# Four changes of order in a two-block layer stack on one Trainium2 core: MLA's keys, the first loads, a norm sum, GLA's outputs

## The chip, the core and the metric

The kernel runs on one core of one Trainium2 chip. The time is that of one execution on the device, in microseconds (us). Three runs of the kernel before took 3557.26, 3553.92 and 3555.59 us; the median is 3555.59.

TensorE multiplies, VectorE (DVE) and ScalarE (ACT) work elementwise, GpSimd (POOL) too, and SyncE (SP) asks for the transfers. Each engine works through its own list in order; between engines there are only semaphores.

## What is computed

One sequence of 256 positions, 2048 channels, float32. Two blocks of two layers each:

```python
for i in range(2):                                   # first block
    z = rmsnorm(x, g_mix[i]) @ w_in[i]               # 4928 columns, in 12 parts
    y_a = mla_group(zq, zkv, zkr, ...)               # 4 heads; q, k of 128 + 64 (rotated), both RMS-normed
    y_b = sc_b * causal_dwconv(sc_c * sc_h, w_sc[i])             # 3 taps
    y_c = silu(layernorm(causal_dwconv(cf_a * sigmoid(cf_g), w_cf[i])))  # 31 taps
    y_d = retention_group(rq, rk, rv, rg, ...)
    x = x + concatenate([y_a, y_b, y_c, y_d]) @ w_o[i]
    uf = causal_dwconv(rmsnorm(x, g_ffn[i]) @ w_up[i], w_ffn_conv[i])    # 2 x 5632 columns
    x = x + (silu(gate) * up) @ w_down[i]
    x = x + (p[i] @ w_pe[i]) * sigmoid(rmsnorm(x, g_pe[i]) @ w_pg[i])
for l in range(2):                                   # second block
    p = rms_norm(x, norm_g) @ w_in                   # forgetting, differential, block and gated linear attention
    x = x + concatenate([fox, diff, moba, gla]) @ w_out
return rms_norm(x, final_norm_g)
```

MLA's queries and keys come from low-rank parts: `c_q = rmsnorm(zq)`, `c_kv = rmsnorm(zkv)`, `q = c_q @ w_q_up`, `kv = c_kv @ w_kv_up`; a key is 128 channels of its head and 64 rotated ones that all heads share, normed together.

## The kernel before

**Slabs.** All lies with channels on the 128 partitions and positions along the row: x is 16 chunks of 128 x 256. A projection is cut into *slabs*: 128 output channels by all input channels, 128 x 2048 numbers, 1 MB. Each float32 operand is used as a rounded high half and a residue. ScalarE rounds a slab (`split_hi`, L1027, tile `whi`), VectorE subtracts (`split_lo`, L1394, tile `wlo`), and TensorE does 16 pairs of matmuls: the high weights by both halves of H (512 columns, L548) and the low weights by H's high half (256 columns, L552). Slabs whose source is not split this way use three matmuls of 256 columns (L550 to L552). H holds the normed input: ScalarE writes its high half (`x_hi`, L1060), VectorE its low half (`x_lo`, L1444). The norm's factor is not in H: the sum over channels is a matmul with ones (`norm_sum`, L586), ScalarE takes the root (`norm`, L1047), VectorE inverts it (`inverse`, L1433) and multiplies every output by it. The squares of x for this sum are made and added by GpSimd, chunk by chunk (`square_sum`, L438 and L443).

**Order.** There is no planner: the order is written out by hand. A slab's turn on each engine is one step of `run`. SyncE loads slab n into one of four places when slab n - 4 is done. In its turn of slab n VectorE first takes the output of slab n from its PSUM bank (L1411 adds the two halves of 512 columns, L1419 multiplies), then makes the residue of slab n + 3 (`AHEAD` is 3), and only then does what hangs on the step number. ScalarE rounds slab n + 3 first. Beside the slabs, the small work of attention hangs on the step s (the slab's number in the layer): on TensorE `behind_first(l, s)` behind slab s and `within_first` in its middle, on ScalarE `beside_first`, on VectorE `before_first` and `after_first` (before and behind the residue). The second block has the same four under the names `after_slab`, `within_slab`, `beside_slab`, `before_split` and `after_split`.

**Steps of the first block.** zq and zkv are s = 0 to 5, zkr 6, cfg 7 to 10, cfa 11 to 14, kv 15, qn 16, qr 17, ret 18 to 25, sc 26 to 37, rg 38 to 41. Behind slab 6 TensorE sums the squares for the low-rank norms (`lora_sums`, L627). Behind qn it sums the keys' squares, ScalarE takes a root, VectorE inverts (`invert(8)`, L1437), and behind qr TensorE spreads the inverse norms over partitions (`spread`, L635); VectorE then scales the keys (`keys_scaled`) and turns the queries (`query_turned`), and the scores of the four heads lie behind slabs 19 to 22. Between these VectorE does 62 steps of two of the four 31-tap convolutions (`cf_taps`, L1532), a few in each slab; GpSimd does the other two (L485, L488) from cfa's third slab on.

**The start.** SyncE asks for x's first quarter, slab 0, x's other three quarters and then slabs 1 to 3. ScalarE rounds slab 0, writes H, and rounds slabs 1 and 2; VectorE follows. `setup` (VectorE) works out the angles of the rotation and the sums for lambda in stages, `set_up` (ScalarE) takes sines and exponentials, `setup_end` finishes.

**pe and pg.** p @ w_pe fills eight banks (`both_units`); ScalarE copies six of them (L1346), VectorE two. Then comes the norm sum and the 16 slabs of pg, in a loop.

**gla.** Behind slabs 13 to 16 and 18 to 21 of the second block TensorE multiplies eight levels of decayed keys and queries (`gla_levels`, first instruction L764), for which VectorE makes differences (L1719), ScalarE two exponentials (`level_exps`, L1204 and L1205) and GpSimd four products (L504, L505). `gla_take` (ScalarE, L1221 and L1222) copies the outputs of the first pair out of four PSUM banks, which the second pair's levels use next.

## Time and profile before

| | |
|---|---|
| median of three runs | 3555.59 us (3553.92 to 3557.26) |
| profiled execution | 3560.03 us, span 3558.2 us |
| mean granted TensorE clock | 0.983 |
| TensorE busy | 97% of the span |
| VectorE, ScalarE, GpSimd busy | 75%, 41%, 28% |
| DMA | 605 MB, mean 170 GB/s |

The span runs from the first to the last instruction. Times of the rows below are us from the start of the span. A busy share is an average over stages with different limits; what counts is where TensorE, which is busy nearly all the time, waits.

### The profile page before, as it was taken

To read this page: it belongs to the slowest core of one execution; us is meant where nothing else is said; L and a number is where in the kernel's file an instruction comes from. 1 tells how busy PE (TensorE), PEld (TensorE's weight loads), DVE (VectorE), ACT (ScalarE), POOL (GpSimd) and SP (SyncE) were. 2 spreads that over 40 slices of the span, in tenths; PEclk is the share of its full clock that TensorE was granted. 3 is DMA by queue.
4 is the path that set the end of the run, shared out by engine and by line. 5 is a ranking of instruction groups with operands and counts; after the bars stand their busy time and mean duration, and the time that the engine had idled before them with its cause. 6 is when DMAs were issued, how large, how long until landed. Compare 5 with 4: busy or idle time off the path is not lost. (4 is left out here: it accounts for less than half of the span.)

```text
span 3558.2 us, 55706 instructions
## 1 busy us (share of the span) xinstructions
PE 3448.0 (97%) x21150; PEld 3027.4 (85%) x21150; DVE 2653.3 (75%) x3438; ACT 1476.1 (41%) x1494; POOL 1008.0 (28%) x794
## 2 busy tenths in 40 slices
PE   6999999999999999999999999999999999999998
PEld 5899888888888888998888888888878888878887
DVE  6876688777786778766887787867767776677775
ACT  3434444343333543344443434335444444444442
POOL 3470433212122434805232121214331004140004
PEclk8999999999999999999999999999999999999999
DMA  4334455555545544344555555555443445444453
GB/s 183 136 132 165 171 189 190 178 195 177 199 171 188 184 171 141 132 156 175 189 189 176 200 174 195 178 187 190 168 154 141 147 174 183 164 145 142 154 178 142
DMA packets 90062, 605.08 MB, mean 170 GB/s; under 512 B 10000, under 2 KB 10160, under 8 KB 28592
## 3 DMA queue, kind: packets, MB, share of 16 engines
q1 hardware_dynamic: 88992, 599.83, 47.9%
q10 hardware_dynamic: 912, 3.12, 0.2%
q8 instruction: 103, 1.69, 0.2%
q14 instruction: 55, 0.45, 0.0%
HBM read 600.81 MB, written 2.10 MB: 169 GB/s over the span
## 5 line engine op out<-in xcount | busy, mean ns | idle before, releaser
L548 PE MATMUL bank<-H,whi 128*128 128x512 f32 x6784 | 2425.6, 401 | 56.4 <-DVE H L1444 40.8
L552 PE MATMUL bank<-H,wlo 128*128 128x256 f32 x7552 | 2130.2, 282 | 0.0
L548 PEld LDWEIGHTS bank<-H,whi 128*128 128x128 f32 x6784 | 1285.3, 189 | 378.1 <-DVE wlo L1394 36.2
L1027 ACT ACTIVATE whi<-raw 128x2048 fp32r<-128x2048 f32 (+1 forms) x610 | 1095.3, 1796 | 1181.9 <-DMA raw<-in_slabs_down 267.3
L1394 DVE TENSOR_TENSOR wlo<-raw,whi 128x2048 fp32r<-128x2048 f32 (+1 forms) x610 | 1338.6, 2195 | 189.8 <-ACT whi L1027 185.8
L552 PEld LDWEIGHTS bank<-H,wlo 128*128 128x128 f32 x7552 | 1441.9, 191 | 0.4
L548 PE MATMUL bank<-G,whi 128*128 128x512 f32 x1408 | 494.6, 393 | 0.0
L465 POOL TENSOR_TENSOR sqtmp<-tmp 128x256 f32<-128x256 f32 x88 | 219.0, 2489 | 891.4 <-DVE tmp L1957 891.4
L552 PE MATMUL bank<-G,wlo 128*128 128x256 f32 x1408 | 398.2, 283 | 0.0
L548 PEld LDWEIGHTS bank<-G,whi 128*128 128x128 f32 x1408 | 264.4, 188 | 61.0
L552 PEld LDWEIGHTS bank<-G,wlo 128*128 128x128 f32 x1408 | 264.7, 188 | 0.0
L1411 DVE TENSOR_REDUCE z<-bank 128x256 f32<-128x512 f32 x148 | 102.1, 690 | 171.1 <-PE bank L552 169.8
L438 POOL TENSOR_TENSOR sqtmp<-x 128x256 f32<-128x256 f32 x135 | 150.0, 1111 | 272.8 <-DVE x L1463 203.8
L443 POOL TENSOR_TENSOR sqacc<-sqacc,sqtmp 128x256 f32<-128x256 f32 x135 | 222.8, 1650 | 10.6
L550 PE MATMUL bank<-H,whi 128*128 128x256 f32 x768 | 224.3, 292 | 0.0
L551 PE MATMUL bank<-H,whi 128*128 128x256 f32 x768 | 218.6, 285 | 0.0
L1411 DVE TENSOR_REDUCE tmp<-bank 128x256 f32<-128x512 f32 x208 | 143.6, 691 | 92.2 <-PE bank L552 90.0
L1462 DVE TENSOR_TENSOR x<-x,bank 128x256 f32 (+1 forms) x192 | 80.8, 421 | 163.6 <-PE bank L552 163.5
L1336 ACT ACTIVATE G<-sqtmp 128x256 f32 (+1 forms) x88 | 36.8, 418 | 400.1 <-POOL sqtmp L465 400.1
L438 POOL TENSOR_TENSOR sqacc<-x 128x256 f32<-128x256 f32 x9 | 17.1, 1895 | 604.1 <-DVE x L1463 558.8
L485 POOL TENSOR_TENSOR sqtmp<-z,cols 128x256 f32<-128x256 f32 (+30 forms) x124 | 120.0, 968 | 191.0 <-DVE z L1905 181.3
L550 PEld LDWEIGHTS bank<-H,whi 128*128 128x128 f32 x768 | 148.6, 193 | 3.8 <-issue 2.7
(314 smaller groups left out, 2503.7 us busy)
## 6 DMA issues: line engine op xcount, KB each, us to landing
raw<-in_slabs_up SPq DMA_DIRECT2D x176, 1024.0 KB, 4.8
raw<-in_slabs_down SPq DMA_DIRECT2D x128, 704.0 KB, 4.1
raw<-in_slabs_wo SPq DMA_DIRECT2D x32, 1024.0 KB, 4.8
raw<-in_slabs_pg SPq DMA_DIRECT2D x32, 1024.0 KB, 4.8
raw<-in_slabs_gates SPq DMA_DIRECT2D x32, 1024.0 KB, 4.8
raw<-in_slabs_wout SPq DMA_DIRECT2D x32, 1024.0 KB, 4.7
raw<-in_slabs_sc SPq DMA_DIRECT2D x24, 1024.0 KB, 4.8
raw<-in_slabs_fox SPq DMA_DIRECT2D x24, 1024.0 KB, 4.8
```

The lines of the kernel that those rows point to most:

```text
L438: pool.tensor_tensor((sqtmp if c else sqacc)[:], x[:, c, :], x[:, c, :], ALU.mult).then_inc(S("pool_sq"), 1)
L443: ins = pool.tensor_tensor(sqacc[:], sqacc[:], sqtmp[:], ALU.add)
L465: pool.tensor_tensor(act_f[:], tmp[:, 3, :], tmp[:, 2, :], ALU.mult).then_inc(S("act_f32"), 1)
L485: pool.tensor_tensor(sqtmp[:, s:T], u[:, 0:T - s], w, ALU.mult).then_inc(S("cf_product"), 1)
L548: pe.matmul(b[0:r.m, :], whi[:, n % RAW, w], r.src[:, k, :], start=at == 0, stop=False)
L550: pe.matmul(b[0:r.m, 0:T], whi[:, n % RAW, w], r.src[:, k, 0:T], start=at == 0, stop=False)
L551: pe.matmul(b[0:r.m, 0:T], whi[:, n % RAW, w], r.src[:, k, T:2 * T], start=False, stop=False)
L552: last = pe.matmul(b[0:r.m, 0:T], wlo[:, n % RAW, w], r.src[:, k, 0:T], start=False, stop=at == r.kt - 1)
L1027: act.activation(whi[:, n % RAW, 0:w], raw[:, n % RAW, 0:w], ACT.Copy).then_inc(S("hi_ready"), 1)
L1394: dve.tensor_tensor(wlo[:, n % RAW, 0:w], raw[:, n % RAW, 0:w], whi[:, n % RAW, 0:w].bitcast(F32), ALU.subtract).then_inc(S("lo_ready"), 1)
L1411: return dve.tensor_reduce(dst, b[0:m, :].rearrange("p (h t) -> p t h", h=2), AX, ALU.add)
L1462: link_in_loop(dve.tensor_tensor(xc, xc, b[:, 0:T], ALU.add), i, j)
```

## The change

1. **MLA.** `spread` and `keys_scaled` move from s = 17 to 18, `query_turned` from 18 to 19, and scores, masks, exponentials, probabilities and outputs of the four heads by one slab. `key_rope`, with its matmul, moves from s = 9 to 13. Four of VectorE's taps leave slab 18.
2. **Start.** Slab 0 is asked for ahead of x. ScalarE squares x in four instructions, VectorE adds them in three, and the norm sum takes four matmuls over y; GpSimd has no part in this first sum. Slab 3 is rounded and split before the first step. p, lambda and positions are loaded into z instead of y. The stages of `setup` hang on s = 2 to 11, one each; ScalarE's `set_up` moves from s = 6 to 12 and `setup_end` from 7 to 13.
3. **pg.** The norm sum, the root and the reciprocal come behind pg's first slab; pg's first four slabs are written out instead of being the loop's first turn.
4. **gla.** ScalarE's `gla_take` comes ahead of `level_exps` in the same step.
5. The packed vectors have 1006 columns instead of 1024.

```diff
@@ SyncE
+        sp.dma_start(raw[:, 0, :], runs[0].slabs[0]).then_inc(S("raw0"), 16)
         for k in range(4):
             sp.dma_start(x[:, 4 * k:4 * k + 4, :].rearrange("p c t -> p (c t)"),
                          d["x"][:, 4 * k * T:(4 * k + 4) * T]).then_inc(S(f"x_in{k}"), 16)
-            if k == 0:
-                sp.dma_start(raw[:, 0, :], runs[0].slabs[0]).then_inc(S("raw0"), 16)
@@ GpSimd
-        square_sum(lambda c: (S(f"x_in{c // 4}"), 16))
@@ TensorE
         def norm_sum():
             k = nth("norm")
-            pe.wait_ge(S("square_sum"), k)
+            if k == 1:
+                pe.wait_ge(S("x_squares"), 3)
+                for c in range(4):
+                    last = pe.matmul(pX[:, 0:T], ones[:], y[:, c, :], start=c == 0, stop=c == 3)
+                last.then_inc(S("norm_sum"), 1)
+                return
+            pe.wait_ge(S("square_sum"), k - 1)
...
+        def gate_norm(l):
+
+            yield
+            pe.wait_ge(S("pe_taken"), 6 * l + 3)
+            pe.wait_ge(S("evac"), by["pe", l].first + 1)
+            norm_sum()
+            yield
...
-            if 21 <= s < 25:
-                weighted(12 + s - 21, 4 * l + 1 + (s - 21) // 2)
+            if 22 <= s < 26:
+                weighted(12 + s - 22, 4 * l + 1 + (s - 22) // 2)
...
-            if s == 9:
+            if s == 13:
                 pe.wait_ge(S("turn_gains"), l + 1)
                 pe.wait_ge(S("evac"), by["zkr", l].first + 1)
                 turn_halves(vtok[:, 0:P], [small[:]], pO)
...
-            if s == 17:
+            if s == 18:
                 spread([((pX, pX, pO, pO)[h][:, (h % 2) * T + t * P:(h % 2) * T + (t + 1) * P], 4 * t + h)
...
-            if 19 <= s < 23:
-                h = s - 19
+                h = s - 20
...
-            pe.wait_ge(S("pe_taken"), 6 * l + 3)
-            pe.wait_ge(S("evac"), by["pe", l].first + 1)
-            norm_sum()
-            run(("pg", l), h_ready(hbase), free=lambda j, l=l: pe.wait_ge(S("pe_taken"), 6 * l + 4 + min(j, 2)))
+            run(("pg", l), h_ready(hbase), gate_norm(l), free=lambda j, l=l: pe.wait_ge(S("pe_taken"), 6 * l + 4 + min(j, 2)))
@@ ScalarE
+            if ahead and isinstance(i, int) and n + 4 * i == AHEAD:
+                return
...
+            if s in (17, 22):
+                gla_take(l, (s - 17) // 5)
             if 16 <= s < 20:
                 level_exps(8 * l + 4 + s - 16)
-            if s in (17, 22):
-                gla_take(l, (s - 17) // 5)
...
         split_hi(r0, 0, 2, 0)
+        for k in range(4):
+            act.activation(y[:, 4 * k:4 * k + 4, :], x[:, 4 * k:4 * k + 4, :], ACT.Square).then_inc(S("x_square"), 1)
+        split_hi(r0, 0, 3, 0)
         norm()
...
-            norm()
             for i, j in run(("pg", l)):
+                if isinstance(i, int) and i == 0 and j == 0:
+                    norm()
@@ VectorE
-                advance(taps, 4 if 4 * i + j in (0, 6, 7) else 0)
+                advance(taps, 4 if 4 * i + j in (6, 7) else 0)
...
-            if l == 0 and s < 6:
-                advance(setting, 2)
-            if l == 0 and s == 5:
+            if l == 0 and 2 <= s < 12:
+                advance(setting, 1)
+            if l == 0 and s == 11:
                 finish(setting)
-            if l == 0 and s == 7:
+            if l == 0 and s == 13:
                 setup_end()
+            if s == 13:
+                key_rope(l)
...
             if s == 9:
-                key_rope(l)
                 lora_low(l)
...
-            if s == 17:
+            if s == 18:
                 keys_scaled(l)
-            if s == 18:
+            if s == 19:
                 query_turned(l)
...
         split_lo(r0, 0, 2, 0)
+        for a, b, n in ((0, 4, 2), (8, 12, 4), (0, 8, 0)):
+            dve.wait_ge(*((S("x_square"), n) if n else (S("x_squares"), 2)))
+            dve.tensor_tensor(y[:, a:a + 4, :], y[:, a:a + 4, :], y[:, b:b + 4, :], ALU.add).then_inc(S("x_squares"), 1)
+        split_lo(r0, 0, 3, 0)
         inverse()
...
-            inverse()
             for i, j, b in run(("pg", l)):
                 k = 4 * i + j
+                if isinstance(i, int) and i == 0 and j == 0:
+                    inverse()
```

## Rows read from the trace of the kernel before

**Rows 1.** The page, busy time, share of the span and instructions of each engine.

```profile
PE 3448.0 (97%) x21150; PEld 3027.4 (85%) x21150; DVE 2653.3 (75%) x3438; ACT 1476.1 (41%) x1494; POOL 1008.0 (28%) x794
```

**Rows 2.** Busy time of each engine from 440 to 1170 us, TensorE's clock, DMA.

```profile
440.00:1170.00 730.00, 730.00 (x4168) 637.06 (x4167) 573.21 (x716) 284.99 (x239) 171.99 (x114) 1.00 0.53 186
```

**Rows 3.** TensorE's waits added up: who for whom, total us, times, longest.

```profile
PE bank L548 <- DVE H L1444: 40.8, 9, 14.4
PE pX L635 <- DVE inv_rms L1437: 17.4, 2, 8.8
```

**Rows 4.** Timelines of the start: start us, length, instruction, idle before and releaser.

```profile
6.28 0.61 POOL L438 TENSOR_TENSOR sqacc<-x 128x256 f32<-128x256 f32 x1 [4.82 <-DMA x<-in_x]
8.87 1.91 ACT L1027 ACTIVATE whi<-raw 128x2048 fp32r<-128x2048 f32 x1 [6.39 <-DMA raw<-in_slabs_zq]
14.43 0.76 PE L548 MATMUL bank<-H,whi 128*128 128x512 f32 x1 [14.43 <-DVE H L1444]
29.22 0.80 PE L548 MATMUL bank<-H,whi 128*128 128x512 f32 x1 [2.01 <-DVE wlo L1394]
43.12 0.59 PE L586 MATMUL pX<-sqacc,ones 128*128 128x256 f32 x2
44.26 1.75 DVE L1433 RECIPROCAL rms<-rms 128x256 f32<-128x256 f32 x1 [12.35 <-ACT rms L1047]
47.12 2.29 DVE L1394 TENSOR_TENSOR wlo<-raw,whi 128x2048 fp32r<-128x2048 f32 x1
49.46 0.80 PE L548 MATMUL bank<-H,whi 128*128 128x512 f32 x1 [5.74 <-DVE wlo L1394]
```

**Rows 5.** TensorE's groups, 43 to 86 us: busy us, mean ns, idle before, releaser.

```profile
L627 PE MATMUL pX<-ones,w 128*128 128x1 f32 x16 | 3.5, 352 | 5.3 <-ACT z L1090 5.3
```

**Rows 6.** Groups by form, 13 to 27.5 us, the first slab.

```profile
L1444 DVE SCALAR_TENSOR_TENSOR H<-x,cols,H 128x256 fp32r<-128x256 f32 x16 | 13.1, 890 | 0.0
L548 PE MATMUL bank<-H,whi 128*128 128x512 f32 x16 | 10.2, 639 | 15.8 <-DVE H L1444 15.2
```

**Rows 7.** Groups by form on VectorE, 1182 to 1189 us, GpSimd idle.

```profile
L1444 DVE SCALAR_TENSOR_TENSOR H<-x,cols,H 128x256 fp32r<-128x256 f32 x16 | 6.4, 478 | 0.0
```

**Rows 8.** Groups by form on TensorE, 305 to 308 us: four matmuls of 256 columns.

```profile
L675 PE MATMUL pX<-z,ones 128*128 128x256 f32 x8 | 1.9, 378 | 0.0
```

**Rows 9.** Groups by form on TensorE, 1331 to 1334.2 us: LoRA sums, layer 1.

```profile
L627 PE MATMUL pX<-ones,w 128*128 128x1 f32 x16 | 1.8, 245 | 0.0
```

**Rows 10.** Timeline of VectorE in MLA of layer 0.

```profile
161.33 0.19 DVE L1437 RECIPROCAL inv_rms<-inv_rms 128x8 f32<-128x8 f32 x1
...
170.77 0.73 DVE L1570 SCALAR_TENSOR_TENSOR z<-z,g_qk,pX 128x512 f32<-128x512 f32 x1
...
179.30 0.69 DVE L1583 TENSOR_TENSOR tmp<-pS,trig 128x512 f32<-128x512 f32 x1
...
182.13 0.19 DVE L1646 RECIPROCAL inv_q<-inv_q 128x8 f32<-128x8 f32 x1
```

**Rows 11.** Timeline of TensorE there: slab 20 starts, and what follows it.

```profile
184.35 0.38 PE L550 MATMUL bank<-H,whi 128*128 128x256 f32 x1
...
190.21 0.49 PE L714 MATMUL pT<-cst,soft 128*128 128x128 f32 x3
```

**Rows 12.** Timeline of VectorE: setup's end, `key_rope`, and a product beside GpSimd.

```profile
97.11 1.43 DVE L1876 TENSOR_TENSOR pT_hl<-y,pT_hl 128x256 fp32r<-128x256 f32 x4
...
109.65 0.48 DVE L1560 SCALAR_TENSOR_TENSOR small<-small,cols,trig 128x256 f32<-128x256 f32 x1
...
135.77 0.92 DVE L1904 TENSOR_TENSOR z<-z,rms 128x256 f32<-128x256 f32 x1
```

**Rows 13.** Timelines of ScalarE and TensorE before pg in layer 0.

```profile
1191.26 1.55 ACT L1346 ACTIVATE z<-bank 128x512 f32<-128x512 f32 x3
1191.95 0.77 PE L548 MATMUL bank<-H,whi 128*128 128x512 f32 x1 [1.63 <-ACT z L1346]
```

**Rows 14.** Timelines of ScalarE and TensorE in gla of layer 0.

```profile
2656.93 0.63 ACT L1204 ACTIVATE tmp<-tmp 128x512 f32<-128x512 f32 x1 [4.41 <-DVE tmp L1719]
2659.03 0.32 PE L764 MATMUL pS<-zeros 1*128 1x384 bf16 x1 [2.31 <-ACT y L1222]
```

More of the change, by code:

```diff
@@ L136, in vector_places @@
     return at, places
+VECTOR_COLUMNS = sum(per * (1 if name == "final_norm_g_2" else L) for name, per in VECTORS)
 def packed_vectors(inputs):
-    packed = np.zeros((P, 1024), np.float32)
+    packed = np.zeros((P, VECTOR_COLUMNS), np.float32)
     for name, l, per, at in vector_places()[1]:
@@ L255, in _build @@
     cst = sb("cst", [P, CONST_W])
-    cols = sb("cols", [P, 1024])
+    cols = sb("cols", [P, VECTOR_COLUMNS])
     ones = sb("ones", [P, P])
@@ L331, in _build @@
         by[key] = Run(d[slab_name(key)], kt, m, count, src, loop, sum(r.count for r in runs))
-        if key[0] == "up" and key[2] == 0:
+        if key[0] == "pg" or key[0] == "up" and key[2] == 0:
             by[key].head = 1
@@ L425, in square_sum @@
         def square_sum(final):
-            if done["norm"]:
-                pool.wait_ge(S("norm_sum"), done["norm"])
             done["norm"] += 1
+            pool.wait_ge(S("norm_sum"), done["norm"])
             if done["g"]:
@@ L478, in _ @@
                 if c == POOL_CF[0]:
-                    pool.wait_ge(S("square_sum"), done["norm"])
+                    if done["norm"]:
+                        pool.wait_ge(S("square_sum"), done["norm"])
                 for s in range(31):
@@ L856, in behind_first @@
                 query_sums(l)
+            if 21 <= s < 25:
+                turn_probs((s - 21) % 2)
             if 20 <= s < 24:
-                turn_probs((s - 20) % 2)
-            if 19 <= s < 23:
-                h = s - 19
+                h = s - 20
                 half = slice(64 * (h % 2), 64 * (h % 2) + 64)
@@ L1101, in beside_first @@
                 last.then_inc(S("root"), 1)
-                if l == 0:
-                    set_up()
+            if s == 12 and l == 0:
+                set_up()
             if 7 <= s < 11:
@@ L1128, in beside_first @@
                 act.activation(inv_q[:], pT[:, 0:8], ACT.Sqrt, bias=eps_q[:]).then_inc(S("query_root"), 1)
+            if 22 <= s < 26:
+                take_o(y[:, s - 22, :])
             if 21 <= s < 25:
-                take_o(y[:, s - 21, :])
+                take_head_probs()
             if 20 <= s < 24:
-                take_head_probs()
-            if 19 <= s < 23:
-                exp_rows((s - 19) % 2)
+                exp_rows((s - 20) % 2)
             if s in (25, 26):
@@ L1391, in split_lo @@
             n = r.first + j + ahead
+            if ahead and isinstance(i, int) and n + 4 * i == AHEAD:
+                return
             w = rr.kt * rr.m
@@ L1603, in before_first @@
         def before_first(l, s):
-            if 19 <= s < 23:
-                dve.wait_ge(S("probs_turned"), 4 * l + max(s - 20, 0))
-                mask_rows((s - 19) % 2, s - 19)
+            if 20 <= s < 24:
+                dve.wait_ge(S("probs_turned"), 4 * l + max(s - 21, 0))
+                mask_rows((s - 20) % 2, s - 20)
             if 27 <= s < 31:
@@ L1646, in after_first @@
                 link(dve.reciprocal(inv_q[:], inv_q[:]))
-            if 19 <= s < 23:
-                probs(None, (s - 19) % 2)
+            if 20 <= s < 24:
+                probs(None, (s - 20) % 2)
             if s in (23, 24):
@@ L1838, in setup @@
             dve.wait_ge(S("const_in"), 16)
-            link(dve.tensor_copy(y[:, 7, :], y[:, 6, :].bitcast(I32)))
+            link(dve.tensor_copy(z[:, 23, :], z[:, 22, :].bitcast(I32)))
             inv = C("inv_freq")
```

22 lines of the change are left out of this document (10 added, 12 removed).

## Prediction

> **What bounds the kernel now.** I read the page's engine lines first, then the busy time of one long stretch, then TensorE's waits added up, and last the timelines of the places where those waits lie. TensorE is busy for 3448 of 3558 us [rows 1], so only what shortens its idle 110 us, or the stretches that it runs at half clock, can move the end. In the long loops nothing does: between 440 and 1170 us TensorE is never idle at a granted clock of 1.00; a pair of matmuls (512 and 256 columns) takes 730/2084 = 0.35 us there, and a slab of 16 pairs 5.6 us [rows 2]. The largest sum of waits is for VectorE's low halves of H, 40.8 us; 14.4 of them are the kernel's first wait. The second is for `inv_rms` in MLA, 17.4 us in two equal stalls [rows 3].
>
> The start is worth more than its waits say. TensorE starts at 14.43, stands still before 29.22 (2.01) and 49.46 (5.74) for a slab's low half, and before the LoRA sums (5.3) [rows 4, 5]. Inside the first slab the pace is not TensorE's: sixteen of VectorE's H instructions take 13.1 us, 0.82 each, while GpSimd squares the same x; in a stretch without GpSimd the sixteen take 6.4, 0.40 each [rows 6, 7]. The matmuls between them took 639 ns for 512 columns [rows 6]: half clock (1.2 GHz) for the most part.
>
> **The start, step by step.** (1) Slab 0 is asked for ahead of x. x's first quarter (0.5 MB) starts GpSimd at 6.28 and the slab (1 MB) starts ScalarE at 8.87 [rows 4]; the vectors (0.5 MB, ScalarE's queue) I take to have landed with the quarter. So 1.1 MB took 2.6 us, 0.43 MB a us, and the flow began near 3.9. Slab and vectors together are 1.5 MB: landed at 7.45. The quarter of x follows at 8.65, before ScalarE has rounded the slab (1.91 us, to 9.35). VectorE's residue of it (2.3 alone) ends at 11.65, and half a us later TensorE starts: 12.2 for 14.43, **gain 2.2**. Ends: 1 (x late) and 3.3 (the slab shares with nothing and lands at 6.3).
> The Trainium skill (Trainium Kernel Development and Optimization, Key Constraints) says that DMAs of the Sync and Scalar queues run on the same 16 engines and interleave. By it the vectors take their share of the time and the gain is 2.2; without it it would be 3.3.
> (2) GpSimd no longer squares x, so x_lo goes at 0.40: done at 11.65 + 6.4 = 18.1, slab 1's residue at 20.4. TensorE is then the slower one in slab 0. I give it 6.7 us at half clock (0.64 a pair, 10.5 pairs) and 5.5 pairs at 0.35: 8.6 us, to 20.8, where it had 12.8: **gain 4.2** (2.4 if all is at half clock). The gap of 2.01 goes: **2.0**. Slabs 1 and 2 took 13.9 us (29.22 to 43.12), the first pairs at half clock behind the gap; without a gap 11.1: **gain 2.8** (0 if the clock falls anyway).
> (3) Behind the rounding of slabs 1 and 2 ScalarE squares x in four instructions of 1024 columns (1.1 us each, half of its 1.91 for 2048 and a little) and VectorE adds in three (1.15, half of a residue); slab 3 is rounded and split behind them, to about 28.3, and TensorE wants it at 33.8. The norm sum is now four matmuls; eight records of four such took 1.9 us [rows 8], the one before 0.59 [rows 4]: **cost 1.3**.
> (4) Slab 3 no longer waits for the root, its reciprocal (1.75), slab 0's reduction and product (1.1) and the residue (43.7 to 49.4, [rows 4]): **gain 5.7**. That chain is now due one slab later, with slab 1's reduction in it: 33.8 + 0.5 + 1.75 + 1.15 + 1.15 + 2.3 = 40.6, and slab 3 ends at 39.4, so 1.2 of it returns. Slabs 3 to 6 took 25.9 (49.46 to 75.34, the first at half clock), now 22.2 + 1.2: **gain 2.5**.
> (5) The rotary angles are worked out a stage a slab in slabs 2 to 11, before two a slab in 0 to 5. VectorE's turn is then 1.1 + 2.3 + at most 1.9 = 5.3, under TensorE's 5.6; zq's last chunk is out at 56.5, its squares (1.7 on ScalarE) at 58.3, slab 6 done at 57.3: a stall of 1.0 for 5.3, **gain 4.3**. The LoRA sums, 24 matmuls of one column, took 5.3 at half clock and 2.8 in layer 1 (16 of them 3.5 and 1.8, [rows 5, 9]): **gain 2.4**.
> Start together: 2.2 + 4.2 + 2.0 + 2.8 - 1.3 + 5.7 + 2.5 + 4.3 + 2.4 = **24.8 us**, ends 16 and 29.
>
> **MLA's keys a slab later.** The stall of 8.7 ends when VectorE, behind 8 taps and a residue, inverts the key norms at 161.33 [rows 10]. Now TensorE runs ret's first slab in that time. But VectorE is never idle from cfa's third slab to here, so the gain is what its chain allows: copy, 8 taps and a residue bring it from 161.5 to 170.8 (where the scaled keys began); ret 0's product 0.4, residue 2.5, scaled keys 3.0; ret 1's product 0.4, residue 2.4, turned queries 3.0 (179.30 to 182.3): 182.5. Scores 0 start then, 0.3 later than before (the slab behind them started at 184.35, [rows 11]), but with one more slab done, 5.9 us: 5.6. From this comes what the change adds to VectorE behind cfa's third slab, where GpSimd's taps have begun: `key_rope`, 1.3 us before, and in layer 0 `setup_end`, 1.9 with its four subtractions at 1.43. Beside GpSimd a product took 0.92 where it is 0.43 else [rows 12], so I bound the two by 1.3 to 2.2 and 1.9 to 3.1. All of it reaches TensorE, the chain having no slack: layer 0 gains 5.6 - 4.1 = **1.5** (0.3 to 2.4), layer 1 5.6 - 1.7 = **3.9** (3.4 to 4.3). Stalls that stay: near 3 us before ret 0 in layer 0, near 4 behind it in both, near 3 before scores 0.
> The Trainium skill (SBUF — State Buffer, Who interferes with whom) gives VectorE and GpSimd an exclusive lock on one port pair, and a VectorE instruction with two SBUF inputs waits for a GpSimd one that reads. It speaks against this move, from a stretch without GpSimd into one full of it: by it the two cost 2.2 and 3.1 and the sum is 1.7 smaller. The 0.92 of [rows 12] is on its side.
> I take off **1.0** for ret's sixth slab, where VectorE now has mask, residue, probabilities and rope together.
>
> **pg's norm sum.** TensorE stands 1.43 us before the sum and 1.63 behind it, both for ScalarE: slab pg 0 needs the bank that ScalarE copies behind a rounding, at 1191.8 [rows 13]. That wait stays, and the sum (0.6), which lay inside it, comes behind slab 0 in the open: **cost 0.6 a layer, 1.2**. Root and reciprocal come 6 us later; VectorE gives slab pg 3's residue near 1207, TensorE wants it near 1211: hidden, by 4 us. Ends: nothing, and 4 a layer if that cover is gone.
>
> **gla.** ScalarE takes the outputs only behind two exponentials, which start at 2656.93 when VectorE's differences are there, after 4.4 idle us; TensorE waits 2.31 for them, up to 2659.03, and as long in layer 1 [rows 14]. The matmuls whose output it is lie in the middle of the slab before, 2.8 us ahead of that wait, and four copies of 0.3 fit into the idle 4.4: **gain 2.3 a layer, 4.6**. Behind it GpSimd's products set the pace of the levels and move up by just as much, so a half-clock stretch gives nothing on top. Ends 2 and 8.
>
> The vectors' 1006 columns for 1024 and pg's first four slabs written out I cost at nothing: 9 KB less, and the same instructions on each engine.
>
> **Sum.** 24.8 + 1.5 + 3.9 - 1.0 - 1.2 + 4.6 = 32.6. The profiled execution took 3560.0 (its span 3558.2 and 1.8 around it): 3527.4. The median of the runs shown is 4.4 below it, 3555.6: **3523**.
>
> **Rivals.**
> x_lo keeps its 0.82 (ScalarE or the transfers set it, not GpSimd): slab 1's residue is at 27.1, so TensorE has gained 2.1 there and nothing in slabs 1 and 2; start 15.7, total 23.5, 3532. Against it: [rows 7] beside [rows 6]. 10%.
> VectorE's added work eats MLA's gain and GpSimd's pace eats gla's: the start less pg's 1.2 and the 1.0, 22.6: 3533. For it: 3.2 to 5.3 us land on the one engine that bounds MLA. 14%.
> All that the edits name goes, half clocks with it: MLA 2 x (8.7 + 0.7 + 1.6) = 22, gla 8, pg 6; with the start 61: 3495. Against it: VectorE's chain, ScalarE's last copy. 4%.
> The other side: every tile laid out behind `cols` starts 72 bytes lower, and VectorE's instructions on them get slower for it. Place: the up and down loops, where VectorE is busy 573 of 730 us [rows 2], 272 of it on such tiles. It binds from 1.58 times their length and outweighs the gains from 1.64; at 1.8 it costs 61 a layer: 3645. Against it: H, ahead of `cols`, and small, behind it, both show 0.48 for an instruction of one shape [rows 7, 12]. 2%.
> Nothing in net: 3556. 2%.
>
> **How the numbers follow.** The forecast has 66%, the rivals 32, unnamed mishaps that end slower 2. Its own range is 3516 to 3530 by the ends above; to hold 8 in 10 it reaches over the two smaller gains: **3513 to 3534**. What a measurement of this kernel can tell from no change is 0.2%, 7 us: faster 0.94, same 0.02, slower 0.04.
>
> **What would show it.** TensorE's first matmul near 12.2, no idle time over 0.3 us up to the norm sum, LoRA sums from near 58 where it was 80.67; H's first sixteen at 0.40 on VectorE. MLA: waits for `inv_rms` near 4, not 8.7, and one for the turned queries near 3. pg: one stall of 3.7. gla: no wait for ScalarE's outputs. It is wrong if the first slab takes over 11 us, if the wait before the LoRA sums is back at 5, or if a stall over 2 us stands in pg's slabs 1 to 3.

## The result, and the profile after

The changed kernel takes 3525.99 us (median of four runs, 3523.16 to 3530.64) where the kernel before took 3556.43 in the same session: ratio 0.9911, 95% interval 0.9899 to 0.9923, which is 27 to 36 us less. The prediction was 3523 with a range of 3513 to 3534. The two profiled executions took 3560.03 and 3530.64 us, 29.4 less; 32.6 were forecast. Each of the two is slower than the median of its kernel by 4 to 5 us, so the traces below are read for where the time goes, the medians for how much it is.

The page's engine line, and the long stretch of [rows 2] again. In that stretch nothing has changed but a wait at its end: pg now begins inside it.

```profile
PE 3441.4 (98%) x21156; PEld 3019.1 (86%) x21156; DVE 2642.3 (75%) x3441; ACT 1467.2 (42%) x1488; POOL 982.2 (28%) x763
```
```profile
440.00:1170.00 730.00, 725.66 (x4177) 635.13 (x4176) 574.57 (x717) 296.73 (x259) 173.41 (x117) 1.00 0.54 187
```

TensorE's waits added up (who for whom: total us, times, longest), against [rows 3]:

```profile
PE bank L549 <- DVE H L1462: 37.6, 6, 12.0
PE bank L549 <- DVE wlo L1412: 10.0, 4, 4.3
PE bank L628 <- DVE z L1928: 5.0, 2, 4.1
PE pX L650 <- DVE inv_rms L1455: 3.6, 1, 3.6
PE pS L721 <- DVE z L1603: 2.6, 1, 2.6
PE pX L642 <- ACT z L1104: 0.2, 1, 0.2
```

The two equal stalls for `inv_rms` (17.4 us) are one of 3.6, in layer 1. A wait has come that was not there before: TensorE's kv unit (L628) stands 4.1 us in layer 0 and 0.9 in layer 1 for VectorE's last output of cfa (L1928). The wait before the LoRA sums is 0.2. No wait for ScalarE's copies of gla's outputs is left; the waits for GpSimd's products there (L792, L800) are 6.4 us for 5.1.

**The start.** Timelines of ScalarE, VectorE and TensorE, against [rows 4, 5]; then the groups of the first slab, 11 to 20 us, against [rows 6].

```profile
7.20 1.91 ACT L1041 ACTIVATE whi<-raw 128x2048 fp32r<-128x2048 f32 x1 [4.72 <-DMA raw<-in_slabs_zq]
11.35 6.42 DVE L1462 SCALAR_TENSOR_TENSOR H<-x,cols,H 128x256 fp32r<-128x256 f32 x16
11.97 0.77 PE L549 MATMUL bank<-H,whi 128*128 128x512 f32 x1 [11.97 <-DVE H L1462]
14.67 0.63 PE L549 MATMUL bank<-H,whi 128*128 128x512 f32 x1
15.83 0.40 PE L549 MATMUL bank<-H,whi 128*128 128x512 f32 x1
20.03 0.50 PE L549 MATMUL bank<-H,whi 128*128 128x512 f32 x1 [0.56 <-DVE wlo L1412]
31.44 1.89 PE L589 MATMUL pX<-y,ones 128*128 128x256 f32 x8
40.13 0.50 PE L549 MATMUL bank<-H,whi 128*128 128x512 f32 x1 [1.26 <-DVE wlo L1412]
57.55 1.92 PE L642 MATMUL pX<-ones,w 128*128 128x1 f32 x16 [0.20 <-ACT z L1104]
60.41 0.77 PE L549 MATMUL bank<-H,whi 128*128 128x512 f32 x1
```
```profile
L549 PE MATMUL bank<-H,whi 128*128 128x512 f32 x16 | 7.3, 485 | 12.0 <-DVE H L1462 12.0
L1462 DVE SCALAR_TENSOR_TENSOR H<-x,cols,H 128x256 fp32r<-128x256 f32 x16 | 6.4, 479 | 0.0
```

The first five pairs of slab 0 start 0.64 us apart, which is half clock, and from the seventh on 0.35: the clock rises in the sixth.

**MLA, layer 0.** VectorE's timeline ahead of the new wait, then TensorE's two waits. VectorE gets to cfa's last output (to 116.8) only behind `setup_end` (109.50 to 112.9) and `key_rope` (112.84 to 114.5), both beside GpSimd's taps: the four subtractions that took 1.43 us [rows 12] take 2.92 here, `key_rope`'s first product 0.82 for 0.48.

```profile
109.50 0.45 DVE L1890 TENSOR_SCALAR neglam<-lamv 128x1 f32<-128x1 f32 x2
109.99 2.92 DVE L1895 TENSOR_TENSOR pT_hl<-z,pT_hl 128x256 fp32r<-128x256 f32 x4
112.84 0.82 DVE L1578 SCALAR_TENSOR_TENSOR small<-small,cols,trig 128x256 f32<-128x256 f32 x1
...
116.08 0.71 DVE L1928 TENSOR_TENSOR z<-z 128x256 f32<-128x256 f32 x1
```
```profile
116.85 0.58 PE L628 MATMUL bank<-cq,whi 128*128 128x256 f32 x1 [4.14 <-DVE z L1928]
160.96 1.32 PE L721 MATMUL pS<-z 128*128 128x128 f32 x5 [2.62 <-DVE z L1603]
```

**Idle time and half clock.** Three stretches that begin at the same work in both kernels: MLA of layer 0 and of layer 1 from the kv unit on (100 us each), gla's levels in layer 1 (90 us). Columns: bounds, length, busy us of TensorE, its weight loads, VectorE, ScalarE, GpSimd, then TensorE's granted clock, DMA share, GB/s. Before, then after:

```profile
133.00:233.00 100.00, 90.60 (x666) 85.83 (x666) 82.01 (x111) 36.96 (x49) 92.10 (x100) 0.93 0.34 118
1380.00:1480.00 100.00, 91.04 (x663) 86.11 (x662) 82.03 (x111) 37.41 (x50) 92.09 (x101) 0.91 0.33 116
3127.00:3217.00 90.00, 84.58 (x882) 71.76 (x881) 64.40 (x88) 40.90 (x49) 37.40 (x30) 0.98 0.40 141
```
```profile
108.00:208.00 100.00, 93.04 (x654) 87.73 (x654) 83.40 (x115) 36.38 (x49) 92.01 (x102) 0.90 0.33 116
1357.00:1457.00 100.00, 94.62 (x706) 89.09 (x705) 86.88 (x115) 38.67 (x50) 92.25 (x99) 0.97 0.35 127
3096.00:3186.00 90.00, 87.96 (x886) 74.71 (x887) 63.09 (x89) 41.18 (x49) 36.79 (x30) 0.94 0.41 141
```

In all three TensorE stands less (2.4, 3.6 and 3.4 us). The granted clock has to be read beside that, and a mean over a stretch misleads, because half clock inside a stall costs nothing. Counting only the half clock in which TensorE worked, by the clock's record in the same traces, it was 9.8 us before and 18.3 after in MLA of layer 0, 10.8 and 6.8 in layer 1, 3.4 and 10.2 in gla; half of that is lost. Idle time and this loss together: 14.3 us before and 16.1 after in layer 0, 14.4 and 8.7 in layer 1, 7.1 and 7.2 in gla. So in this pair of traces the gain in idle time of MLA layer 0 and of gla layer 1 does not show in the time.

**pg, layer 0.** ScalarE, then TensorE, against [rows 13]:

```profile
1164.49 1.89 ACT L1041 ACTIVATE whi<-raw 128x2048 fp32r<-128x2048 f32 x1
1166.29 1.54 ACT L1361 ACTIVATE z<-bank 128x512 f32<-128x512 f32 x3
```
```profile
1167.12 0.77 PE L549 MATMUL bank<-H,whi 128*128 128x512 f32 x1 [4.34 <-DVE wlo L1412]
1175.38 0.59 PE L593 MATMUL pX<-sqacc,ones 128*128 128x256 f32 x2
```

From the end of `both_units` to slab 0 it is 4.34 us, where it was 3.74 with the sum in it (1188.21 to 1191.95); layer 1 has 3.85 for 3.57. The sum stands in the open behind slab 0. ScalarE's copy and VectorE's residue now end within 0.3 us of each other (1166.8 and 1167.06), so the wait is for both, and the profile names the later one.

**Where the 29.4 us came from**, by the same point of the work in both traces: the kv unit of layer 0 starts 25.0 earlier (133.30, 108.30); the last loop of layer 0's MLA block ends 23.4 earlier (429.88, 406.47), so MLA lost 1.6; the end of `both_units` is 25.4 earlier and the end of pg 23.4 (1284.15, 1260.77), so pg cost 2.0; MLA of layer 1 brought 5.5 (28.9 at 1561.74), pg of layer 1 cost 0.7, gla brought 1.7 in layer 0 and lost 0.8 in layer 1 (30.3 and 29.8 at its ends). Loops that are the same in both kernels shift too: the 25.4 is 2.0 more than the 23.4 ahead of it, and in layer 1 the lead falls from 28.9 to 24.5 us in the up loop and is back at 29.3 at the end of the down loop (last section). So single terms of one pair of traces are good to some 2 us, and to less where a long loop lies between the two points. The terms named add up to 27.1 us; the other 2.3 come from loops that the change doesn't touch.

### The profile page after: what moved, and what is told of

It is laid out like the page before. It is cut to its first block and busy times, and to the rows that moved or that the text cites. A ratio compares the mean times of both kernels' runs of the same rounds, so it can differ in the third digit from the quotient of the medians.

```text
span 3528.8 us, 55547 instructions
## 1 busy us (share of the span) xinstructions
PE 3441.4 (98%) x21156; PEld 3019.1 (86%) x21156; DVE 2642.3 (75%) x3441; ACT 1467.2 (42%) x1488; POOL 982.2 (28%) x763
## 5 line engine op out<-in xcount | busy, mean ns | idle before, releaser
L444 POOL TENSOR_TENSOR sqacc<-sqacc,sqtmp 128x256 f32<-128x256 f32 x120 | 211.9, 1765 | 9.4
L439 POOL TENSOR_TENSOR sqtmp<-x 128x256 f32<-128x256 f32 x120 | 133.0, 1108 | 269.9 <-DVE x L1481 207.4
```

The lines of the kernel that those rows point to most:

```text
L439: pool.tensor_tensor((sqtmp if c else sqacc)[:], x[:, c, :], x[:, c, :], ALU.mult).then_inc(S("pool_sq"), 1)
L444: ins = pool.tensor_tensor(sqacc[:], sqacc[:], sqtmp[:], ALU.add)
```

## Experiments

Each kernel was timed in turn with the kernel before. The column "against after" is the difference of the ratios times 3556; it is uncertain by some 6 us between sessions and by less inside one, so of the single experiments only start alone, MLA's chain back, gla back, taps out of cfa and the last three differ from after by more than that. The kernel after was timed in a session of its own. The kernel before took 3556.8 us in the session of the first four experiments, 3560.9 in that of the next four and 3558.0 in the last.

| run | median us | ratio to before, 95% interval | against after |
|---|---|---|---|
| after | 3526.0 | 0.9911 (0.9899, 0.9923) | |
| start alone | 3544.8 | 0.9966 (0.9952, 0.9979) | +20 |
| MLA's chain back | 3539.6 | 0.9955 (0.9941, 0.9969) | +16 |
| pg back | 3525.3 | 0.9915 (0.9902, 0.9929) | +1 |
| gla back | 3533.9 | 0.9934 (0.9920, 0.9947) | +8 |
| GpSimd squares x too | 3535.1 | 0.9928 (0.9911, 0.9944) | +6 |
| slab 0 behind x | 3526.1 | 0.9908 (0.9891, 0.9924) | -1 |
| taps out of cfa | 3519.5 | 0.9884 (0.9867, 0.9900) | -10 |
| setup and rope at 12 | 3525.4 | 0.9901 (0.9885, 0.9918) | -4 |
| rope at 9 in layer 1 | 3526.6 | 0.9911 (0.9898, 0.9925) | 0 |
| taps + setup | 3515.4 | 0.9882 (0.9867, 0.9897) | -10 |
| taps + setup + pg back | 3512.3 | 0.9874 (0.9859, 0.9889) | -13 |
| best | 3506.9 | 0.9859 (0.9844, 0.9874) | -18 |

### The start alone

```diff
-            if s == 18:
+            if s == 17:
                 spread([((pX, pX, pO, pO)[h] ...
...   (keys scaled at 17, queries turned at 18, scores behind 19 to 22, taps in slab 18;
...    pg and gla as before; key_rope and setup_end stay at s = 13)
```

> The changed kernel with three of its four parts put back: MLA's chain a slab earlier (spread behind slab 17, scores behind 19 to 22, with VectorE's four taps in slab 18), pg's norm sum ahead of its first slab, gla's outputs behind the exponentials. What is left is the new start, with setup_end and key_rope at s = 13. If the parts add up as predicted, it gains the start's 24.8 us and loses what the two pieces of VectorE's work at s = 13 cost (4.1 in layer 0, 1.7 in layer 1): 19.0 less than the kernel before, 3537. By what the trace after shows (LoRA sums 23.1 earlier, slab 7 25.4 earlier, VectorE's two pieces 5.1 us in layer 0 and all of it on the path) it is 3536 too. The rival, that the two pieces at s = 13 are hidden as long as MLA's chain is not moved, gives 3531. In the trace: slab 7 starts near 60.4; the wait for inv_rms in layer 0 is 5.0 or more, beside a wait of about 4 in the kv unit.

3544.8: 12 less than before (7 to 17 by the interval), not 19; the two profiled executions are 17.6 apart. The kv unit is reached at 112.1 us (112.7 after), so the start is not at fault. Waits of TensorE in this kernel:

```profile
PE pX L650 <- DVE inv_rms L1457: 19.3, 2, 10.4
PE bank L628 <- DVE z L1930: 5.1, 2, 4.2
```

The rival (hidden) falls: beside 8.9 and 10.4 us for `inv_rms`, more than the 8.7 and 8.8 of before, stand the kv unit's 4.2 and 0.9 and waits of 0.6 and 1.2 before the scores. In layer 0 that is 13.8 us for 9.4, in layer 1 12.5 for 8.8. So the work put at s = 13 costs 4.4 us of idle time in layer 0, of its 5.1, and 3.7 in layer 1, where only `key_rope` (1.7) moved. Idle time isn't the whole price. TensorE works less at half clock in layer 1 than before (4.9 us for 10.8), and from the kv unit to the next norm sum layer 1 takes 310.6 us for 308.9, 1.7 more; layer 0 takes 314.3 for 308.4.

### MLA's chain a slab back

```diff
-            if s == 18:
+            if s == 17:
...   (as in the run above; start, pg and gla as in the kernel after)
```

> The changed kernel with only MLA's chain put a slab back (spread behind slab 17, keys scaled there, queries turned at 18, scores behind 19 to 22, four taps in slab 18); key_rope and setup_end stay at s = 13. The prediction gave the shift itself 5.6 us a layer and took 1.0 off for ret's sixth slab: without it 10.2 more than the kernel after, 3536. The traces of before and after show smaller differences: TensorE's idle time in layer 0 9.4 before and 6.8 after with VectorE 4 us further behind, in layer 1 8.8 and 5.3; by them the shift is worth 4 to 5 us a layer less half clocks, so 3533. If the shift only moves the wait about, 3527. In the trace: layer 1's wait for inv_rms near 8 to 9, layer 0's 5 to 6, the 4 us in layer 0's kv unit unchanged.

16 us slower than after by the ratios (9 to 22), where the prediction's step gives 10.2 and the trace theory 7. The wait for `inv_rms` (layers 0 and 1 together, longest 10.4) is back:

```profile
PE pX L650 <- DVE inv_rms L1455: 16.9, 2, 10.4
```

All MLA waits: 12.0 against 6.8 in layer 0 and 12.5 against 5.3 in layer 1, 12.4 us of idle time. Half clock goes the other way: outside the waits it cost 6.7 and 4.3 us here, 9.1 and 3.4 after, so idle time and half clock together give 10.6 us, 2.6 of it in layer 0 and 8.0 in layer 1. The shift is therefore worth about what was predicted; the time of 16 doesn't contradict that. What spoiled MLA's net is the work moved to s = 13.

### pg's norm sum back ahead

```diff
-            run(("pg", l), h_ready(hbase), gate_norm(l), ...
+            pe.wait_ge(S("pe_taken"), 6 * l + 3)
+            pe.wait_ge(S("evac"), by["pe", l].first + 1)
+            norm_sum()
+            run(("pg", l), h_ready(hbase), ...
```

> The changed kernel with only pg put back: the norm sum ahead of pg's first slab. The prediction priced this part at 0.6 us a layer, the sum in the open behind slab 0: 1.2 less than the kernel after, 3525. The traces of before and after show from the end of both_units to the start of slab 0 3.74 before and 4.34 after in layer 0 (3.57 and 3.85 in layer 1), although the sum has left that stretch, and a half clock twice as long behind it in layer 0: by them the part cost 2.2 and 0.7, so 2.9 less, 3523. If it is worth what its wording suggests (the sum hidden behind slab 0), the kernel gets slower by 1 to 2 us, 3527.

No difference that can be told (ratio 0.9915). In the trace the two waits and the sum between them are back, 4.2 us in all from 1160.17 to slab 0, against 4.34 and 0.59 behind the slab:

```profile
1162.34 0.67 PE L593 MATMUL pX<-sqacc,ones 128*128 128x256 f32 x2 [2.17 <-ACT z L1364]
1164.39 0.76 PE L549 MATMUL bank<-H,whi 128*128 128x512 f32 x1 [1.39 <-ACT z L1364]
```

This kernel has the same code as after up to there, and the stretch takes as long, with the sum inside it (layer 1: 3.84 against 3.85). So nearly all of the 0.6 and 0.3 us by which the stretch is longer after than before is not the change's; its price there is the sum in the open, 0.6 a layer as forecast. Put back on top of two other edits (below) it gave 3.1 us of median. From the end of `both_units` to the end of pg the nine traces with the sum behind slab 0 take 96.1 and 95.6 us in the mean (94.8 to 98.0), the five with it ahead 94.8 and 94.2 (92.8 to 95.9): 2.7 us for both layers, more than the sum itself. Some 1.0 of it is half clock in pg (2.0 and 1.9 us lost for 1.6 and 1.3); why there is more of it is open.

### gla's outputs behind the exponentials again

```diff
-            if s in (17, 22):
-                gla_take(l, (s - 17) // 5)
             if 16 <= s < 20:
                 level_exps(8 * l + 4 + s - 16)
+            if s in (17, 22):
+                gla_take(l, (s - 17) // 5)
```

> The changed kernel with only gla_take put back behind the two exponentials. Prediction: the stall of 2.3 us a layer before the second pair's first level comes back, 4.6 more than the kernel after: 3530.6. Rival, from the traces: in both layers the stall is gone after the change, but TensorE then stands for GpSimd's products 1.2 us in the levels of the second pair and in layer 1 at half clock for two slabs instead of one; net gain 1.9 and 0.1, so 3528. In the trace: two waits near 2.3 for ScalarE's outputs.

8 us slower, by its interval 2 to 15: the prediction's 4.6 is inside, the rival's 2 at the edge. The two stalls are back, one a layer:

```profile
PE pS L779 <- ACT y L1234: 4.6, 2, 2.3
```

### GpSimd squares x as well

```diff
+        for c in range(DC):
+            pool.wait_ge(S(f"x_in{c // 4}"), 16)
+            ...
+            pool.tensor_tensor((sqtmp if c else sqacc)[:], x[:, c, :], x[:, c, :], ALU.mult) ...
+            if c:
+                pool.tensor_tensor(sqacc[:], sqacc[:], sqtmp[:], ALU.add) ...
```

> The changed kernel in which GpSimd squares and adds x at the start as it did before, besides; its sums are not used. Only GpSimd's company is added. Prediction: GpSimd is what held VectorE's H instructions at 0.82 us instead of 0.40. Then the sixteen take about 13 us again instead of 6.4, the first slab 12 to 13 instead of 7.5, slab 1's residue comes 6 to 7 us later, and the three adds of the squares are slower too: 6 to 8 us more than the kernel after, 3533. Rival: the pace was set by ScalarE's writing of H or by the arrival of x, which the change moved too: then the sixteen stay near 0.40 and the time at 3526.

The first slab, 11 to 25 us, same groups as above:

```profile
L1474 DVE SCALAR_TENSOR_TENSOR H<-x,cols,H 128x256 fp32r<-128x256 f32 x16 | 13.1, 892 | 0.0
L561 PE MATMUL bank<-H,whi 128*128 128x512 f32 x16 | 9.7, 609 | 14.4 <-DVE H L1474 13.8
```

The sixteen take 13.1 us, as in the kernel before, and 6.4 without GpSimd. The LoRA sums start at 66.49 for 57.55, 8.9 later. The time is 6 us longer by the ratios, which alone are not clear of nothing; but the next run, of the same session and with the start 1.4 us slower than after, took 3526.1, and all four of its executions (3524.4 to 3530.4) are shorter than all four of this kernel (3533.7 to 3537.8). GpSimd's company doubles the time of these instructions. The rival (ScalarE or the transfers) is refuted.

### Slab 0 behind x's first quarter

```diff
-        sp.dma_start(raw[:, 0, :], runs[0].slabs[0]).then_inc(S("raw0"), 16)
         for k in range(4):
             sp.dma_start(x[:, 4 * k:4 * k + 4, :] ...
+            if k == 0:
+                sp.dma_start(raw[:, 0, :], runs[0].slabs[0]).then_inc(S("raw0"), 16)
```

> The changed kernel with slab 0 asked for behind x's first quarter, as before. Prediction: the order alone is worth 2.2 us (ends 1 and 3.3), all of it at TensorE's first matmul: 14.4 where the kernel after has 12.0, total 3528. Rival: what follows (ScalarE's rounding, H) swallows it, and the matmuls of the first slab run closer together for starting later: 3526 to 3527, slab 0 ending near 20.

The time doesn't tell the two apart. The first matmul does:

```profile
13.37 0.77 PE L550 MATMUL bank<-H,whi 128*128 128x512 f32 x1 [13.37 <-DVE H L1463]
```

It is 1.4 later than with the new order, and so are the LoRA sums (58.93). The order is worth 1.4 of the 2.5 us that the first matmul gained; the other 1.1 are a residue and a first low half of H without GpSimd (2.29 us for 2.72, and 0.4 for 0.8) and a slab that lands 0.3 earlier.

### Twelve taps out of cfa

```diff
-                if c:
-                    advance(taps, 4)
...
             for i, j, b in run(("sc", l), None, 26):
-                advance(taps, 3)
+                advance(taps, 4)
```

> The changed kernel with VectorE's 12 taps of slabs 12 to 14 (cfa) taken out there and done in sc instead, four a slab instead of three. Theory: all of MLA's stalls are VectorE's arrears, so it does not matter which of its work is taken ahead of the kv bank; 4 of these taps (2.7 us) and the part of 4 more that is not idle time lie ahead of it, and 4 (3.2) between it and the inverse of the key norms. The wait in the kv unit falls from 4.1 to under 1 in layer 0 and from 0.9 to nothing in layer 1, layer 1's wait for inv_rms from 3.6 to under 1, that for the scores from 2.6 to under 1: 8 to 12 us less, 3516. Rival: the bank or the chain of squares and roots over ScalarE sets these waits: then they stay, and sc gets slower: 3526 to 3530.

10 us less by the ratios, where 8 to 12 were expected; 7 less than the run before, of the same session, whose start is 1.4 slower. Waits for cfa's output, `inv_rms` and the turned queries, both layers:

```profile
PE pS L721 <- DVE z L1603: 4.7, 2, 3.1
...
PE bank L628 <- DVE z L1928: 1.8, 1, 1.8
PE pX L650 <- DVE inv_rms L1455: 1.1, 1, 1.1
```

MLA's waits fall from 6.8 and 5.3 to 4.5 and 3.1, without the chain of scores being touched: they are VectorE's arrears. sc does not get slower, as the rival had it: in 90 us of it TensorE is busy for 88.7, after for 88.8. The waits don't go where expected, and not by as much as the work taken off (7.9 us in layer 0): part of what the kv unit and `inv_rms` no longer show turns up before the scores of layer 1 (3.1).

### setup_end and key_rope a slab earlier

```diff
-            if s == 12 and l == 0:
+            if s == 11 and l == 0:
                 set_up()
...
-            if l == 0 and s == 13:
+            if l == 0 and s == 12:
                 setup_end()
-            if s == 13:
+            if s == 12:
                 key_rope(l)
```

> The changed kernel with ScalarE's set_up at s = 11 and setup_end and key_rope (with its matmul) at s = 12, a slab before GpSimd's taps begin. Theory: beside GpSimd they took 3.4 and 1.7 us, without it 1.9 and 1.3: the four subtractions are back near 1.4 us in all, VectorE is 1.9 us earlier at the kv bank in layer 0 and 0.4 in layer 1, TensorE waits about 2.2 there instead of 4.1: 2.3 less than the kernel after, 3524. Rival: the two pieces cost the same anywhere, since VectorE has no slack from slab 8 on: 3526, the wait in the kv unit stays at 4.1.

The four subtractions, now ahead of GpSimd's taps, and the waits:

```profile
101.34 1.43 DVE L1895 TENSOR_TENSOR pT_hl<-z,pT_hl 128x256 fp32r<-128x256 f32 x4
```
```profile
PE pX L650 <- DVE inv_rms L1455: 4.8, 2, 3.2
...
PE bank L628 <- DVE z L1928: 3.1, 2, 2.5
```

1.43 us for 2.92, and the kv unit waits 2.5 for 4.1, as the theory has it. The time is 4 us less by the ratios, a difference whose interval includes zero.

### key_rope back at 9 in layer 1

```diff
-            if s == 13:
+            if s == (13, 9)[l]:
                 key_rope(l)
```

> The changed kernel with key_rope and its matmul back at s = 9 in layer 1 alone. Prediction: at s = 13 it costs layer 1 1.7 us of VectorE's time beside GpSimd, and all of it reaches TensorE; so 1.7 less than the kernel after, 3524, with layer 1's waits (0.9 in the kv unit, 0.8 in ret's first slab, 3.6 for inv_rms) together 1.7 shorter. By the start alone against the kernel before (waits in layer 1's MLA of 12.5 against 8.8 us, the move of key_rope being the only difference there) it is 3 us or more: 3522. Rival: VectorE's place at s = 9 is as full as at 13 and TensorE pays the same elsewhere: 3526.

The time doesn't move. In the trace layer 1's waits in the kv unit and in ret's first slab are gone and the last one is 3.47: 3.5 for 5.3, so 1.8 less idle time, the prediction's 1.7. But it is not in the time of layer 1 either: half clock outside the waits costs 5.1 us for 3.4, and from the kv unit to the next norm sum layer 1 takes 304.1 us, in the five traces with `key_rope` at 13 and the same chain 303.0 to 305.4. In layer 0, whose code is the same, the kv unit waited 5.2 this time for 4.1.

```profile
PE bank L628 <- DVE z L1928: 5.2, 1, 5.2
```

### Both edits, pg back, and a best version

```diff
-                if c:
-                    advance(taps, 4)
...
-            if l == 0 and s == 13:
+            if l == 0 and s == 12:
                 setup_end()
...   (both edits above in full)
```

> The changed kernel with both edits at once: VectorE's 12 taps out of cfa and into sc, and set_up at s = 11, setup_end and key_rope at 12. Theory (VectorE's arrears are one sum, whatever they are made of): alone the first gave 0.27% and the second 0.10% against the kernel after; together they give what is left of the waits, in layer 0 4.5 us after the first alone, of which the second takes 1.9, in layer 1 3.1, of which it takes 0.4 to 1.3: 11 to 13 less than the kernel after, 3514. Rival: the waits left after the first edit belong to the chain of scores (roots and sums over ScalarE), not to arrears: then nothing beyond the first edit, 3517 to 3519.

3515.4. No wait is left in MLA of layer 0 but 1.7 before the scores; layer 1 has 1.4 and 1.6. The ratio (0.9882) is hardly below that of the taps alone (0.9884, measured in another session), so the time does not show the second edit; the waits do in layer 0 (1.7 us for 4.5), and in layer 1 they stay (3.0 for 3.1).

```diff
+            norm_sum()
+            run(("pg", l), h_ready(hbase), ...
...   (and the two edits of the run before)
```

> The kernel of the run before this one with pg's norm sum back ahead of its first slab. Prediction's price of that part: 1.2 us, so 1.2 less than without this edit, 3513. By the traces it was 2.9: 3511. The run that put back pg alone gave 0.7 less with an interval that holds 0 and 4. Rival: nothing or slower, 3514 to 3515.

3512.3, 3.1 less than its neighbour of the same session; the interval of each is 5 us wide to either side, so the time alone doesn't show it.

```diff
-            if s == 12:
+            if s == (12, 9)[l]:
                 key_rope(l)
...
+                if c == 1 and l:
                     advance(taps, 4)
...
-                    advance(taps, 8)
+                    advance(taps, 6 if l else 7)
```

> A version meant to beat both: the kernel of the run before this one, with key_rope back at s = 9 in layer 1, layer 1's first four taps in slab 12 (ahead of GpSimd's), and fewer taps in kv, qn and qr (7 each in layer 0, 6 in layer 1, before 8); what is missing is done when sc's ninth slab begins. VectorE is then 1.6 to 4.8 us earlier in the chain up to the scores: TensorE's waits in MLA, about 2.5 us in layer 0 and 1.5 to 3 in layer 1 by then, fall below 1 us each: 3 to 5 less than the run before, 3508. Rival: what is saved there comes back in sc, where four leftover taps stand in one slab and VectorE has 0.2 to 0.5 us a slab to spare: 3512.

3506.9, ratio 0.9859: 0.52% below the kernel after, 1.4% below the kernel before, and its interval (up to 0.9874) ends below that of after (from 0.9899). TensorE's busy time and clock in MLA of layers 0 and 1, 100 us each from the kv unit on:

```profile
102.00:202.00 100.00, 99.50 (x744) 94.23 (x742) 83.02 (x112) 40.81 (x53) 90.19 (x95) 0.97 0.39 134
1340.00:1440.00 100.00, 99.73 (x751) 94.73 (x750) 81.11 (x108) 40.56 (x52) 92.17 (x100) 0.97 0.39 138
```

99.5 and 99.7 us busy, at a clock of 0.97 where it was 0.93 and 0.91 before. sc did not give it back: from the kv unit to the next norm sum, sc included, layer 0 takes 299.4 us and layer 1 299.4, in the run before this one 300.7 and 302.9.

## Why the prediction was right, step by step

Each change of place can be priced from all fourteen traces, because each part stands in some kernels in the old order and in some in the new: the time between the same two matmuls, in the mean over the kernels of either kind. For the start, and for the two pieces of work moved to s = 13, the old kind is the one trace of the kernel before, with the chance that lies in a single trace.

| part | forecast, us less | the pair of traces | means over the traces |
|---|---|---|---|
| start, up to the kv unit | 24.8 | 25.0 | 25.6 |
| MLA layer 0, chain a slab later | 5.6 | | 4.4 |
| MLA layer 0, work moved to s = 13 | -4.1 | both: -1.6 | -5.6 |
| MLA layer 1, chain a slab later | 5.6 | | 6.7 |
| MLA layer 1, work moved to s = 13 | -1.7 | both: 5.5 | -2.1 |
| both layers, for ret's sixth slab | -1.0 | no wait there | in the rows above |
| pg, both layers | -1.2 | -2.7 | -2.7 |
| gla, both layers | 4.6 | 0.9 | 7.0 |
| sum | 32.6 | 27.1 | 33.3 |

A mean is good to 1 or 2 us. That the sum comes out within 1 us is in part luck: the forecast had pg 1.5 too cheap and MLA 1.0 too good, and the start 0.8 and gla 2.4 too small.

**Start, 24.8.** By slab 7 it was 25.4 (85.78 to 60.41), by the kv unit 25.0. The terms: first matmul 2.5 (2.2 forecast, of which the order is 1.4); slab 0 7.5 us for 12.8, 5.3 (4.2), because the clock rose earlier than assumed: the forecast had ten and a half of its pairs at half clock, five and a half were; its 512 columns took 485 ns in the mean, not 639; the gap behind it 1.5 of 2.0, since 0.56 stay, where the forecast allowed no idle time over 0.3; slabs 1 and 2 2.5 (2.8); the norm sum 0.9 (1.3) dearer; the gap before slab 3 5.7 (5.7); slabs 3 to 6 1.5 (2.5), with the 1.26 before slab 4 that the prediction had as 1.2; the wait before the LoRA sums 5.1 (4.3); the sums 2.2 (2.4). Single terms were off by up to 1.1 us either way and cancelled. That x_lo's pace is GpSimd's doing is shown (squares twice).

**MLA.** From the kv unit to the next norm sum layer 0 takes 308.4 us before, 314.0 with the old chain and the work at s = 13 (two traces), and 309.6 with the new chain (six traces); layer 1 308.9, 311.0 and 304.3 (five). The mechanism is as forecast, the layers are not alike: the shift is worth less in layer 0. The size of the moved work was near its upper bound: 3.4 and 1.7 us, 5.1 in all, for the 4.1 taken (3.2 to 5.3). The waits that "stay" were misplaced: I looked for them at ret and passed over the kv unit, which needs the bank of cfa's last output and is the first to meet VectorE's arrears. That it is arrears is shown: fewer taps, an earlier setup and an earlier rope each shorten them, and with all three they are gone. In layer 0 the shift and the moved work together saved 2.6 us of idle time (9.4 to 6.8), and more half clock took it back; the prediction had priced no half clock there. The Trainium skill (SBUF — State Buffer, Who interferes with whom) says that a VectorE instruction with two SBUF inputs contends with a GpSimd one that reads SBUF, and one with at most one such input, outside the modes that use both ports, does not. The trace agrees: `setup_end`'s four subtractions, with two SBUF inputs, took twice their time beside GpSimd, 2.92 for 1.43, and VectorE's reduction out of PSUM took 0.69 in either company.

**pg, 1.2.** Layer 0 cost 2.0 by the pair of traces, layer 1 0.7. The sum is in the open as said, the one stall is 4.3 and 3.9 for the 3.7 forecast, and no stall stands in slabs 1 to 3. What the forecast had at nothing is what comes on top of the sum, in part half clock (the run with pg back).

**gla, 4.6.** The stall is gone in both layers and comes back with the old order, 2.3 each. From the first level of the first pair to the first level of the second TensorE takes 37 us in every trace with the new order and 39 to 40 in the three with the old, 2.3 to 2.8 a layer. In this pair of traces it brought only 1.7 and -0.8 in all: in layer 1 there was more half clock (0.94 for 0.98), and the slower pace of the tail cost 1.6 us (below). The run with pg back has the same code in gla and no half clock at all from 3010 us to its end. From norm sum to norm sum the eleven traces with the new order take 502.4 us in layer 0 (499.4 to 504.7), the three with the old 507.5 (506.9 to 508.1); layer 1 to the end 494.1 and 496.0, where single traces lie up to 5 us apart. That is 7 us, and 8 (2 to 15) by the run that undid it. Beyond the stall, the old order has more half clock in the levels of layer 0, 10 to 14 us in its three traces and 0 to 10, 3.7 in the mean, in the eleven with the new; the forecast's "a half-clock stretch gives nothing on top" is its step that does not hold there. Layer 1 shows no such gain.

## What to carry to other kernels

On the engine that feeds TensorE, arrears are passed on from one due output to the next: work taken off ahead of the first of them shortens the later waits, and work that is added there was paid in full here (5.6 us for 5.1, 2.1 for 1.7). VectorE's short pieces of set-up with two inputs in SBUF took up to twice as long beside GpSimd's taps, so place them before GpSimd starts. Look for the first place where a buffer must be free, not for the place where the old stall was. Read idle time and granted clock together: an idle microsecond saved counts only if the clock does not fall elsewhere, and half clock inside a stall costs nothing. One pair of traces doesn't price a term of 2 us; the same stretch in all kernels that share its order does.

## What the hardware showed that was not expected

Matmuls of one shape at a granted clock of 1.00 have two paces. SyncE's four issues in the last loop of the second block, one a slab: 16.97 us less one issue of 0.33 over three slabs is 5.55 a slab in the kernel before, and 17.29 gives 5.65 after.

```profile
3406.27 16.97 SPq L406 DMA_DIRECT2D raw<-in_slabs_gates  x4
```
```profile
3375.54 17.29 SPq L408 DMA_DIRECT2D raw<-in_slabs_gates  x4
```

Both paces stand in each of the fourteen traces, in stretches of some tens to some hundreds of us, and change places between kernels and within loops; between 3323 and 3450 us this alone cost the kernel after 1.6 us. In the up loop of layer 1 it cost 4.4: TensorE is busy for all of 200 us in both kernels, with 1156 matmuls before and 1134 after.

```profile
1700.00:1900.00 200.00, 200.00 (x1156) 176.34 (x1155) 173.89 (x219) 82.67 (x72) 61.74 (x37) 1.00 0.53 190
```
```profile
1672.00:1872.00 200.00, 200.00 (x1134) 173.36 (x1133) 170.62 (x213) 82.15 (x72) 60.87 (x36) 1.00 0.52 184
```

So unchanged loops shift by up to some 4 us. That it is also why single executions of one kernel lie 7 us apart is likely, but not shown: each kernel has one trace. What sets the pace is open.

The clock fell to 1.2 GHz in stretches where TensorE had not stood: in the kernel after at 3176 us, 23 us behind its last wait (0.5 us, at 3153), and in the best version in MLA at 120 and 137 us, while its one wait in those 100 us (0.5) came at 186. It worked through the first of these stretches too:

```profile
120.00:123.50 3.50, 3.50 (x19) 3.50 (x19) 3.40 (x6) 1.31 (x3) 3.27 (x4) 0.51 0.62 262
```

What brought the clock down there is open.
